# Row sums of squares partly added on GpSimd: five products with a matrix of ones leave TensorE, five additions join GpSimd

## The reference, cut to what matters

```python
y = y.reshape(bsz, s, SSD_D) * jax.nn.silu(z_s.astype(f32))
y = rms_norm(y.reshape(bsz, s, SSD_GROUPS, SSD_D // SSD_GROUPS),
             ssd_norm_w.reshape(SSD_GROUPS, SSD_D // SSD_GROUPS))

def rms_norm(x, w):
    xf = x.astype(jnp.float32)
    y = xf * lax.rsqrt(jnp.mean(xf * xf, axis=-1, keepdims=True) + EPS)
    return (y * w.astype(jnp.float32)).astype(x.dtype)
```

## Time and profile before

| | before |
|---|---|
| median of 3 runs | 1641.02 us |
| lowest and highest run | 1640.03 and 1642.58 us |
| span of the profiled execution | 1638.3 us |
| PE busy | 1599.2 us (98%) |
| PE weight loads busy | 1316.2 us (80%) |
| DVE busy | 938.6 us (57%) |
| ACT busy | 675.8 us (41%) |
| POOL busy | 163.7 us (10%) |

### The profile page before, as it was taken

One profiled execution on the slowest core, in us unless ns is written; L12 is line 12 of the kernel. 1 busy time (PEld: TensorE's weight loads), 2 busy tenths in 40 slices (PEclk: granted clock), 3 DMA queues, 4 the chain that ended last, 5 costly groups with the idle time before them and its releaser, 6 DMA issues.

```text
span 1638.3 us, 21431 instructions
## 1 busy us (share of the span) xinstructions
PE 1599.2 (98%) x8303; PEld 1316.2 (80%) x8303; DVE 938.6 (57%) x1397; ACT 675.8 (41%) x1167; POOL 163.7 (10%) x186
## 2 busy tenths in 40 slices
PE   7999999999999999999999999999999999999998
PEld 6877878778888777878888788877787888888886
DVE  5678758856735677766534538565556533333334
ACT  5464456453324433343433445444444422232321
POOL 2012215310001000000000124311000000000000
PEclk9999999999999999999999999999999999999999
DMA  7344223221052986633324132222124233332222
GB/s 195 91 119 127 65 84 97 78 55 51 27 218 90 310 242 231 244 116 90 124 90 141 29 93 76 73 72 65 54 89 129 64 90 102 90 102 92 101 94 72
DMA packets 195401, 179.10 MB, mean 109 GB/s; under 512 B 5982, under 2 KB 175021, under 8 KB 192244
## 3 DMA queue, kind: packets, MB, share of 16 engines
q1 hardware_dynamic: 191888, 169.56, 33.8%
q10 hardware_dynamic: 2276, 6.95, 1.2%
q0 software_dynamic: 1152, 1.44, 0.5%
HBM read 173.58 MB, written 4.58 MB: 109 GB/s over the span
## 4 chain that ended last, share of the span: by engine, by line
PE 72%; DVE 1%; ACT 1%; issue 1%; POOL 0%; DVEq 0%; ACTq 0%
PE acc L656 12%; PE acc L657 12%; PE acc L658 12%; PE acc L697 7%; PE acc L698 7%; PE acc L699 7%; PE acc L1215 2%; PE acc L1217 2%; PE acc L712 2%; PE acc L710 2%; PE acc L711 2%; PE acc L1216 2%; PE acc L1359 1%; PE acc L1343 1%; PE acc L750 1%
## 5 line engine op out<-in xcount | busy, mean ns | idle before, releaser
L2121 DVE TENSOR_TENSOR w_low<-w_raw,w_high 128x1024 fp32r<-128x1024 f32 x230 | 283.7, 1235 | 543.1 <-ACT w_high L1438 542.7
L1438 ACT ACTIVATE w_high<-w_raw 128x1024 fp32r<-128x1024 f32 x224 | 237.3, 1059 | 657.4 <-PE acc L658 405.9
L656 PE MATMUL acc<-h_high,w_high 128*128 128x512 f32 (+1 forms) x1248 | 488.4, 391 | 7.9 <-DVE w_low L2121 2.3
L658 PE MATMUL acc<-h_high,w_low 128*128 128x512 f32 (+1 forms) x1248 | 480.0, 385 | 0.0
L657 PE MATMUL acc<-h_low,w_high 128*128 128x512 f32 (+1 forms) x1248 | 479.7, 384 | 0.0
L656 PEld LDWEIGHTS acc<-h_high,w_high 128*128 128x128 f32 x1248 | 235.2, 188 | 68.9 <-issue 16.7
L658 PEld LDWEIGHTS acc<-h_high,w_low 128*128 128x128 f32 x1248 | 235.0, 188 | 46.9
L657 PEld LDWEIGHTS acc<-h_low,w_high 128*128 128x128 f32 x1248 | 235.4, 189 | 45.9 <-issue 1.7
L697 PE MATMUL acc<-w_high,act_high 128*128 128x512 f32 x496 | 193.7, 390 | 3.6 <-DVE arena L2847 1.5
L699 PE MATMUL acc<-w_high,act_low 128*128 128x512 f32 x496 | 193.0, 389 | 0.0
L698 PE MATMUL acc<-w_low,act_high 128*128 128x512 f32 x496 | 193.0, 389 | 0.0
(11 more groups left out here) (394 smaller groups left out, 1977.8 us busy)
## 6 DMA issues: line engine op xcount, KB each, us to landing
w_raw<-w_in SPq DMA_DIRECT2D x68, 512.0 KB, 3.9
w_raw<-w_mlp SPq DMA_DIRECT2D x64, 512.0 KB, 4.0
w_raw<-w_up SPq DMA_DIRECT2D x44, 512.0 KB, 4.0
arena<-w_ada SPq DMA_DIRECT2D x13, 1024.0 KB, 8.2
w_raw<-w_out SPq DMA_DIRECT2D x24, 512.0 KB, 3.3
early<-w_ada SPq DMA_DIRECT2D x11, 1024.0 KB, 6.2
w_raw<-w_down SPq DMA_DIRECT2D x22, 512.0 KB, 3.3
w_raw<-w_branch_gate SPq DMA_DIRECT2D x16, 512.0 KB, 4.1
```

The source lines that it names most:

```text
L656: pe.matmul(out_, wh, xh, start=start, stop=False)
L658: return pe.matmul(out_, wl, xh, start=False, stop=stop)
L1438: f(WH[:, off % 2, :], RAW[:, off % 4, :], ACT.Copy).then_inc(sem("w_high"), 1)
L2121: tt(WL[:, off % 2, :], RAW[:, off % 4, :], WH[:, off % 2, :].bitcast(F32), ALU.subtract).then_inc(sem("w_low"), 1)
```

## The change

Instead of summing each square tile on PE, GpSimd adds tiles 1, 2 and 3 of a group into tile 0 with `y_add` (a tensor_tensor of 128x512 in fp32), where it can. The first group is then one product with ONE (`y_sums(0, 0, True)`). In the second group tiles 5 and 6 are added into tile 4, and tile 7 keeps a product of its own (`y_sums(1, 4, False)` and `y_sums(1, 7, True)`). The square tiles are now one for tile 0 of a group and one shared by the three others, so `y_squares(i)` waits until GpSimd has read the tile before.

```diff
         def y_square_of(i):
 
-            return FT[:, C0 + i % 2, :]
+            return FT[:, C0 + (i % 4 > 0), :]
...
-            def y_sums(i):
+            def y_sums(g, i, last):
 
                 pe.wait_ge(sem("y_square"), i + 1)
-                pe.matmul(PS[:, 6 + i // 4, :], ONE, y_square_of(i), start=i % 4 == 0, stop=i % 4 == 3)\
-                    .then_inc(sem("y_sum"), 1)
+                if i % 4 == 0:
+                    pe.wait_ge(sem("y_added"), [3, 5][g])
+                m = pe.matmul(PS[:, 6 + g, :], ONE, y_square_of(i), start=i % 4 == 0, stop=last)
+                if last:
+                    m.then_inc(sem("y_sum"), 1)
...
             pe.wait_ge(sem("d_gram_out"), 8)
-            y_sums(0)
             gated(3)
-            y_sums(1)
             gated(4)
-            y_sums(2)
             gated(5)
-            y_sums(3)
+            y_sums(0, 0, True)
             gated(6)
-            y_sums(4)
             gated(7)
-            y_sums(5)
             merge_in_32()
             gated(8, [0])
-            y_sums(6)
+            y_sums(1, 4, False)
             for part in range(4):
                 merge_out_32(part)
                 gated(8, ks=[4 + part])
-            y_sums(7)
+            y_sums(1, 7, True)
...
                 act.wait_ge(sem("z_step"), i + 1)
-                if i > 1:
-                    act.wait_ge(sem("y_sum"), i - 1)
+                if i == 4:
+                    act.wait_ge(sem("y_sum"), 1)
+                elif i > 1:
+                    act.wait_ge(sem("y_added"), i - 1 if i < 4 else i - 2)
...
-                act.wait_ge(sem("y_sum"), 4 * g + 4)
+                act.wait_ge(sem("y_sum"), g + 1)
...
+            def y_add(i):
+
+                pool.wait_ge(sem("y_square"), i + 1)
+                if i % 4 > 1:
+                    pool.wait_ge(sem("y_added"), i - 1 if i < 4 else i - 2)
+                pool.tensor_tensor(y_square_of(0), y_square_of(0), y_square_of(i), ALU.add).then_inc(sem("y_added"), 1)
+
...
+            y_add(1)
             for i in range(3, 8):
                 z_times(i)
+                if i != 5:
+                    y_add(i - 1)
             pool.wait_ge(sem("z_step"), 8)
+            pool.wait_ge(sem("y_added"), 5)
             pool.wait_ge(sem("d_blocks"), 1)
```

## The result

| | before | changed |
|---|---|---|
| median (20 runs each, on one chip) | 1640.14 us | 1643.38 us |
| lowest and highest run | 1635.92 and 1642.58 us | 1639.78 and 1647.90 us |
| span of the profiled execution | 1638.3 us | 1643.9 us |
| POOL busy | 163.7 us | 171.7 us |

The ratio is 1.0025, with a 95% interval of 1.0018 to 1.0033. The change made the kernel 3.2 us slower by the medians, 4.1 us by the ratio. The forecast was 4.0 us and "slower". The median lies inside the predicted range, 0.4 us above its lower end, but outside the narrower range of the forecast itself (1644.2 to 1645.9). About 0.9 us of the distance to 1645.0 is the starting point: the forecast added its 4.0 us to 1641.0, the median of 3 runs, and 20 runs of the same kernel have 1640.14.

A forecast was written before the change was run, and what follows sets the result against it. The prediction took DVE's elimination chain, which sets the start of `merge_in_32`, as the bound. Products 0, additions 3.96 and clock 0 gave about +4.0 us on 1641.0, so 1645.0 us; range 1643.0 to 1647.6.

The forecast's parts named there:

- What bounds the kernel: Before `merge_in_32`, an unbroken DVE chain sets the merge's start, although PE is busy 98% of the span.
- rival 5: Before `merge_in_32`, PE is the limit after all: faster by 4.25 us, 1636.8 us; chance 0.05.
- Five products, credited 0: On PE before `merge_in_32`, five removed products of 0.85 us, 4.25 us together, only become longer waits: 0 gained.
- Four additions meet the chain at 0.99 us each, 3.96: In DVE's elimination, four of POOL's five additions each hold a step 0.99 us: 3.96 us; the fifth costs 0.
- Rival 2: In the elimination, only three additions meet DVE's chain: 3.0 us, 1644.0 us; chance 0.11.
- rival 3: In the elimination, each addition costs DVE its whole length: 5.2 us, 1646.2 us; chance 0.10.
- rival 4: In the elimination, DVE doesn't stand still under an addition: 0 us, 1641.0 us; chance 0.07.
- Neighbours add no price: Where POOL instructions stand back to back, DVE gets a turn between two, so adjacency adds no further cost.
- PE's waits: PE waits some 7.5 us for L2121, before `gated(5)`, `gated(6)` and `gated(7)`, and about 1.8 us before `merge_in_32`.
- The clock behind the merge, credited 0: No clock dip behind `merge_in_32`, 0 us; a granted clock below 1 just behind it would fail the prediction.
- rival 1: The clock dips at the wait before `merge_in_32`: another +1.6 us, 1646.6 us; chance 0.22.
- Past the merge, all moves by the same amount, and nothing later gives it back: From `merge_in_32` to the end, both traces run in parallel, so the delay of about 4.0 us stays.

The follow-up runs named there:

- e2: The changed kernel with each GpSimd addition replaced by a one-column memset, sums of squares incomplete; 1638.34 us, ratio 0.9988 to the kernel before.
- e6: The changed kernel itself, unedited, run again for a second profile; 1642.48 us, ratio 1.0017 to the kernel before.
- e11: The changed kernel itself, unedited, profiled a third time; no run time given, 19.15 us from `merge_in_32` to `merge_in_64`.
- e1: The kernel before, all products kept, plus five GpSimd additions reading a constant tile twice into an unused tile; 1643.25 us, ratio 1.0012.
- e3: The changed kernel with each addition replaced by two write-only 128x512 memsets, sums of squares incomplete; 1639.52 us, ratio 0.9997 to the kernel before.
- e9: The kernel before, unedited, profiled a second time; span 1638.4 us, 18.4 us from `merge_in_32` to `merge_in_64`.
- e4: The kernel before with `z_times` for tiles 2 to 6 moved from POOL to DVE; 1637.57 us, ratio 0.9980.
- e8: The kernel before with only the second group's two additions, the first group keeping its four products; 1639.17 us, ratio 1.0001.
- e5: The changed kernel with four unused filler products before `gated(5)` and one before the merge; 1642.75 us, ratio 1.0028 to the kernel before.
- e10: The kernel before, unedited, profiled a third time; no run time given, 18.8 us from `merge_in_32` to `merge_in_64`.

## Why the prediction was right, step by step

**What bounds the kernel: right.** DVE's chain set the start of the merge. Without the products (e2) the merge stayed where it was, and rival 5 has fallen with it.

**Five products, credited 0: right up to the merge.** 4.0 of 4.25 us became waits (e2).

**Four additions meet the chain at 0.99 us each, 3.96: right.** Exactly the four named did, and the chain grew by 3.83 us, 0.96 each. e6 had 3.78 and e11 3.86. Rival 2 (three additions) and rival 3 (the whole length of 1.3 us or more) have fallen. So has rival 4: e1 shows the hold without the products, e3 its absence without the reading. For the rule that rival 3 took at its word, this stretch gives 0.96 us where an addition that starts at once takes 1.31 to 1.43 us: the DVE step already under way goes on.

**Neighbours add no price: right.** POOL ran three instructions back to back from 303.17, and DVE got one step in at each boundary.

**PE's waits: right before the merge, wrong in sum and place.** I had 7.5 us for the splits: 3.7 us before `gated(5)`, 2.3 before `gated(6)` and 1.5 before `gated(7)`. The first was 4.40, since the hold under `z_times(4)` fell on the split L2121 itself (2.17 us instead of 1.22), and `gated(4)` waited 0.72. The rows have no other, which makes 5.1 us: in the slow clock `gated(5)` ended so late that `gated(6)` no longer waited, and `gated(7)`, at 325.61, came only 0.14 us behind the end of its split. So part of the forecast waiting was spent in slower products. Before the merge it was 1.66 us (forecast 1.8), and the merge started at 332.97 (forecast 333.29). The dip in `gated(5)` was absorbed, as the prediction said, although it held for most of the block (0.50 in the window from 312 us).

**The clock behind the merge, credited 0, with rival 1 at +1.6: wrong.** The rival's mechanism occurs: all three profiles of the changed kernel had the dip, and it cost 2.9 us, not 1.6. By its own sign the prediction fails here, in those executions that have the dip. I had sized it by the stretch from 126 to 130 us in the earlier trace rows; here the low clock lasted about twice as long. In the runs it comes and goes: 10 of the 20 runs of the changed kernel had a mean clock of 0.994 or less (mean 1646.0 us) and 10 were above (1641.7 us); of e6's 12 runs, 4 and 8. That the lower clock of those runs lies at this place is likely by the profiles, but only profiles show places, and other places dip too (near 126 us and 1280 us in most of the kernels, 540 us in some). Such a dip has its own price: the kernel before has one near 1280 us, e9 has none, and e9, 1.4 us behind at `merge_in_64`, has nearly the same span (1638.4 against 1638.3 us).

**"Past the merge, all moves by the same amount, and nothing later gives it back": wrong.** This is the other step that failed. The kernel before loses 0.9 us, or over 2 us with a dip, in a gap inside `merge_out_32`, and the change loses that gap. The earlier trace rows end before it, and I did not look past it: the 98% of the page had hidden it.

So the total came out right by two errors that cancel, and that is luck. How well they cancel is an estimate, from differences of profiles and the share of runs with a low clock. For the means it is 3.8 us for the chain, less the gap, plus 2.9 us times the share of executions with a dip. The three profiles of the kernel before put the gap at 0.9, 2.2 and 2.6 us, 1.9 us on average. With a share of a half, as in the 20 runs, this gives 3.4 us (4.4 with the cheapest gap), and with a third, as in e6, 2.9 us (3.9). Measured were 4.1 us (3.0 to 5.4) by the ratio of the 20 runs and 2.8 us (1.0 to 4.6) by that of e6. Both agree, and neither is a sharp test. The 10 runs without a low clock say the same: their mean is 1.9 us above that of the kernel before (1639.8 us), half of what the chain lost.

**What stays open.** Whether the gap is a wait for instructions, as the table makes likely; I made no kernel for it. It is not the number of products alone, since PE runs the same instructions in e1 and e4 as in the kernel before. Nor is it known why the same wait of 1.6 us ends with a dip in some executions only, and no profile shows an execution of the changed kernel without one.

## What to carry to other kernels

Ask of each piece of work that is to go to GpSimd what DVE is doing then. If DVE is running short two-input instructions in SBUF, and the end of that chain is waited for, GpSimd's reading instruction costs the chain most of its own length (0.96 of some 1.4 us); here DVE did the same multiplication in less time than it lost. Work taken off a 98% busy engine is gained only where no other engine's chain ends last: before the merge four additions for five products cost 3.8 us; behind it one for one shortened the stretch by about a product, though the times do not resolve it. And look for clock and gaps in the next stages too, because a wait that costs nothing itself can lower the clock of the work behind it.

## What the runs showed of the hardware

- POOL instructions that only write SBUF (memsets of 0.53 us) cost DVE's chain 0.08 us in all, for the eight that met it; a POOL addition that reads one tile twice held it 0.74 us (e1), and one that reads two tiles 0.96 us (the change).
- Behind waits of 1.55 to 1.66 us (e6, e8, the change and e11) the granted clock fell to 1.2 GHz in the small products of the merge; behind 0.51 to 0.73 us (e1, e2, e3, e5) it did not. Inside `merge_out_32` it fell behind gaps of 1.02 to 1.29 us (e5, e9, e10) and not behind 0.74 us (before). The earlier trace rows have 1.68 us with no dip, behind which stood products of 128x512. One dip here cost 2.9 us.
- PE can stand still for 0.7 to 1.3 us in a run of 32x32 products with no releaser that the profile shows, and whether it does changes with edits elsewhere. In six profiles the product at that place started 1.3 to 1.6 us after a 16 KB transfer of kind "instruction" had ended.
